# GpSimd splits the first expert's down weights, and VectorE's last two up pieces go behind the block table

## The reference

```python
h = rms_norm(x, norm_mix_g)
qa, ka, va, qb, kb, vb, gates = split(h @ w_in)
ya = swa_sink_attention(qa, ka, va, ...)      # banded, 8 heads
yb = stick_breaking_attention(qb, kb, vb)     # causal, 8 heads
x  = x + (gate_a * (ya @ w_proj_a) + gate_b * (yb @ w_proj_b)) @ w_out
h2 = rms_norm(x, norm_ffn_g)
# top group of 4, then top 2 of its 8 experts
# assignments sorted by expert, each expert padded to blocks of 128 rows
yb = (silu(xr @ w1[e]) * (xr @ w3[e])) @ w2[e]   # for each block of 128 rows
x  = x + segment_sum(yb * row_weight)
```

## Time and profile before

| | |
|---|---|
| median of 3 runs | 2684.91 us (2681.92 to 2688.1) |
| the profiled execution | 2685.95 us, span 2684.1 us |
| TensorE busy | 2586.1 us, 96% of the span |
| VectorE busy | 1638.4 us, 61% |
| ScalarE busy | 1490.5 us, 56% |
| GpSimd busy | 612.9 us, 23% |
| DMA | 536.67 MB, mean 200 GB/s |

### The profile page before, as it was taken

How to read it: one execution, slowest core, us unless ns; L and a number is a source line. 1 busy time by engine, 2 the same in 40 slices (tenths; PEclk the granted TensorE clock), 3 DMA queues, 4 the chain that set the end, 5 groups by cost and what they waited for, 6 DMA issues and landing times. The chain is left out here.

```text
span 2684.1 us, 41247 instructions
## 1 busy us (share of the span) xinstructions
PE 2586.1 (96%) x13573; PEld 2158.1 (80%) x13574; DVE 1638.4 (61%) x2216; ACT 1490.5 (56%) x2628; POOL 612.9 (23%) x707
## 2 busy tenths in 40 slices
PE   7999999989999999999899999699999999999997
PEld 6788777678888888888789998577788888888886
DVE  4400555478777777777543433588766677766673
ACT  4312777567767667676421211358666677766663
POOL 0000111144444444444000000022211222221221
PEclk9999999999999999999899999799999999999999
DMA  6454434586575556543644344479977789877782
GB/s 186 124 206 147 125 127 129 152 273 222 191 215 176 179 185 191 186 149 103 205 164 126 126 126 129 173 274 389 324 231 241 246 277 320 323 236 227 227 303 65
DMA packets 197344, 536.67 MB, mean 200 GB/s; under 512 B 20136, under 2 KB 70776, under 8 KB 192736
## 3 DMA queue, kind: packets, MB, share of 16 engines
q1 hardware_dynamic: 170576, 432.80, 47.1%
q0 software_dynamic: 26640, 102.18, 13.5%
HBM read 403.37 MB, written 131.53 MB: 199 GB/s over the span
## 5 line engine op out<-in xcount | busy, mean ns | idle before, releaser
L1078 POOL TENSOR_TENSOR sb_sig<-sb_sig,sb_R 128x512 f32<-128x512 f32 (+1 forms) x320 | 341.2, 1066 | 410.2 <-DVE sb_R L1018 409.9
L52 PE MATMUL ex_ps_h<-w_region,ex_x_hi 128*128 128x512 f32 x816 | 322.1, 395 | 0.8 <-DVE ex_x_lo L1934 0.8
L54 PE MATMUL ex_ps_h<-w_region,ex_x_lo 128*128 128x512 f32 x816 | 318.3, 390 | 0.0
L53 PE MATMUL ex_ps_h<-w_region,ex_x_hi 128*128 128x512 f32 x816 | 317.9, 390 | 0.0
L1939 DVE TENSOR_TENSOR w_region<-ex_w,w_region 128x1024 fp32r<-128x1024 f32 x248 | 284.7, 1215 | 1.4 <-ACT w_region L1787 1.3
L1018 DVE TENSOR_TENSOR_SCAN sb_R<-sb_z,sb_R,sb_zeros 128x512 f32<-128x512 f32 x192 | 245.6, 1279 | 57.8 <-ACT sb_z L946 57.6
L1944 DVE TENSOR_TENSOR ex_wd_lo<-ex_w,ex_wd_hi 128x1024 fp32r<-128x1024 f32 x200 | 239.3, 1218 | 40.8 <-ACT ex_wd_hi L1794 40.7
L1787 ACT CAST w_region<-ex_w 128x1024 fp32r<-128x1024 f32 x248 | 239.8, 1052 | 8.2 <-DMA ex_w<-in_w_exp 8.2
L958 ACT CAST sb_aT_hi<-sb_pst 128x512 fp32r<-128x512 f32 (+1 forms) x320 | 168.3, 526 | 134.1 <-PE sb_pst L1107 130.8
L1026 DVE TENSOR_TENSOR sb_aT_lo<-sb_pst,sb_aT_hi 128x512 fp32r<-128x512 f32 (+1 forms) x320 | 192.1, 601 | 51.9 <-ACT sb_aT_hi L958 49.8
L945 ACT ACTIVATE sb_sig<-sb_z 128x512 f32<-128x512 f32 (+1 forms) x320 | 172.4, 539 | 85.7 <-PE sb_z L1100 84.3
(11 more groups left out here) (296 smaller groups left out, 6164.4 us busy)
## 6 DMA issues: line engine op xcount, KB each, us to landing
ex_w<-in_w_exp SPq DMA_DIRECT2D x378, 512.0 KB, 9.3
sb_w_hi<-wg_d SPq DMA_DIRECT2D x48, 512.0 KB, 3.6
sb_w_lo<-wg_d SPq DMA_DIRECT2D x48, 512.0 KB, 4.5
gates<-sb_go SPq DMA_DIRECT2D x64, 256.0 KB, 4.0
mo_gates<-gates SPq DMA_DIRECT2D x64, 256.0 KB, 4.1
h<-w_stage POOLq DMA_DIRECT2D x17, 512.0 KB, 2.9
nt_x<-in_x SPq DMA_DIRECT2D x16, 512.0 KB, 4.1
vhl<-nt_vo SPq DMA_DIRECT2D x16, 512.0 KB, 5.1
```

Of the source, the lines that this page charges most:

```text
L52: nc.tensor.matmul(out, w_hi, x_hi, start=first, stop=False)
L53: nc.tensor.matmul(out, w_hi, x_lo, start=False, stop=False)
L54: return nc.tensor.matmul(out, w_lo, x_hi, start=False, stop=last)
L1078: nc.gpsimd.tensor_tensor(sig[:, j % 5, 0:width], sig[:, j % 5, 0:width], R[:, r, first:first + width], ALU.mult).then_inc(a_done, 1)
```

## The change

The four splits of the first expert's down pieces move from VectorE to GpSimd, where they stand between `fetch(0)` and `fetch(1)`. Up piece 6 moves behind `split_x(0)` and the table, in front of up piece 7. VectorE gets one wait, for all four down splits, in front of the loop. The low halves have the same values as before.

```diff
@@ gpsimd
             pool.wait_ge(table_step, FIRST_COLUMN)
             fetch(0)
+            for k in range(KF):
+                pool.wait_ge(down_rounded, k + 1)
+                nc.gpsimd.tensor_tensor(wd_lo[:, 0, k, :], wr[:, KD + k, :], wd_hi[:, 0, k, :],
+                                        ALU.subtract).then_inc(down_split, 1)
             pool.wait_ge(table_step, TABLE)
             pool.wait_ge(x_turned, 1)
             fetch(1)
@@ vector
-            first_up(NEARLY)
             split_x(0)
             table()
-            for j in range(NEARLY + 1, KD):
+            for j in range(NEARLY, KD):
                 first_up(j)
-            for k in range(KF):
-                down_piece(0, 0, k)
+            dve.wait_ge(down_split, KF)
             dve.wait_ge(table_step, BOUNDS)
             all_experts(dve, up_weights, rows)
```

## The result

The changed kernel takes 2697.82 us (median of 5 runs, 2695.46 to 2698.65) against 2684.81 us (5 runs of the kernel before beside it): ratio 1.0046, 95% interval 1.0035 to 1.0056. It is slower: the medians differ by 13.0 us, and the ratio stands for 12.4 us. I had forecast 4.4 us and a range up to 2692.5.

What follows compares the result with a forecast made beforehand. Expert 1's last down piece landing was taken to bind; with turns, block 0 starts +4.9 us, last issue +3.7, landing 1775.5 against 1771.08: +4.4 us on 2684.91, 2689.3 us; range 2683.5 to 2692.5.

Steps and rivals of the forecast that it cites:

- What bounds the kernel, and that a shift at 1775 carries to the end: DMA engines, then TensorE, are full from 1775 on, so a shift of that beginning moves the end as much.
- The exclusion, from one VectorE split of 1.19 us in another stage: Stick-breaking stage: a split beside a GpSimd product took 1.19 us instead of 0.67, so two-input VectorE instructions and GpSimd reads exclude.
- The rival without contention: One-hots and products run side by side unhindered; only the order acts, -0.7 us, 2684.2 us; chance 0.14.
- So they don't share, they take turns: One-hots and GpSimd's products alternate, an instruction at a time; block 0 starts 4.9 us later; chance 0.58.
- The rival in which GpSimd keeps the turn: Four products run in one piece, 1748.05 to 1755.25, before the third L1921; +6.4 us, 2691.3; chance 0.12.
- 1.80 us a product: Each waiting 128 x 1024 GpSimd product: 1.93 us extrapolated from smaller sizes, less 0.13 of start-up; 2.2 at the upper end.
- Landing, from the last issue at 1767.0 to 1775.5, 0.7 us more than before: Expert 1's last down piece: six loads at 400 GB/s, 7.9 us, gather 1.3, first data 2.0, scatter-add to 1775.5.
- Up piece 6 behind the table costs nothing on TensorE but costs in SyncE's queue: Up piece 7 is delayed 1.14 us, harmless to TensorE; expert 1's up piece 6 load joins the down pieces' burst.
- The second gather and the new wait on VectorE have slack: Second gather goes out some 5 us later with 6 us to spare; VectorE's new wait is met before reached.

Runs made afterwards that it cites:

- pool_only: Changed kernel with up piece 6 back at its old place, so only the down splits move to GpSimd; ratio 1.0037 to the kernel before.
- resync: Changed kernel with one wait between GpSimd's gather and its four queued products, none between the products; ratio 1.0036 to the kernel before.
- pool_memset: Kernel before plus four GpSimd memsets behind the first gather, VectorE's first down split waiting for them; ratio 1.0001 to the kernel before.
- pool_late: Changed kernel with GpSimd's four products held until VectorE has written the fourth one-hot pair; ratio 1.0012 to the kernel before.
- gaps_no_add: Kernel before with up pieces 6, 7 and down pieces 0, 1 split in VectorE's idle gaps, without the empty block's scatter-add; ratio 0.9992.
- swap_in: Changed kernel with the two inputs of VectorE's wide one-hot product exchanged; ratio 1.0060 to the kernel before.

## Why the prediction was wrong

- *What bounds the kernel, and that a shift at 1775 carries to the end:* right here. `turn_g(1)` moved by 13.0 us, the end by 13.7.
- *The exclusion, from one VectorE split of 1.19 us in another stage:* right, and it is the main cause: pool_only, with the products alone, loses 8.9 of the 13.7 us. The rival without contention fell.
- *"So they don't share, they take turns":* this step failed. Behind the gather there were no turns, and one one-hot waited for all four products (11.04 us). The two products of the earlier trace rows each had idle time in front of them; no row showed queued ones against VectorE, so the step from "one waits" to "they alternate" had nothing under it. The rival in which GpSimd keeps the turn came true, in a stronger form than I priced: the instruction that was already issued was held too, although I had put it first because it began 0.16 us earlier. The rule that I quoted, whichever is second waits, did not hold here by the recorded starts. My two reasons against this rival (VectorE's instruction has waited since its issue, GpSimd needs its start-up) did not help VectorE. Of the 9.3 us by which block 0 started late 2.6 are this step, the difference to resync.
- *1.80 us a product:* too little. Four queued products take 9.24 us, 2.31 each; +2.0 us for the four. The estimate of 2.25 us, half of what the Trainium skill (GPSIMD Engine Reference, "3.1 Elementwise — side-by-side cycle accounting") gives for an addition of 2048 elements, was nearer than my extrapolation from 128 and 512 elements. The 0.13 us that I took off for a product that waited had no row behind it: the one of the earlier trace rows needed 1.15 us after the split's end, more than its 1.09 alone. resync, which takes turns as I had it, starts block 0 6.7 us late instead of 4.9, and most of these 1.8 us are the longer products.
- *Landing, from the last issue at 1767.0 to 1775.5, 0.7 us more than before:* the other large miss. I counted bytes at 400 GB/s and gave the scatter-add 0.5 us. It came to 5.3 more than before: 3.2 for the scatter-add, and 2.1 for the rest of the burst. Even with turns the kernel would have lost about 10 us (resync: 951.7 against 941.4), not 4.4. So the direction was right, and the sum failed at three places: no turns, longer products, a later landing.
- *Up piece 6 behind the table costs nothing on TensorE but costs in SyncE's queue:* right in kind; 1.1 us of issue alone. The end is 1.7 us later, but `turn_g(1)` only 0.7, and block 0 began at the lower clock in that profile.
- *The second gather and the new wait on VectorE have slack:* right, neither is on the chain.

## What to carry to other kernels

Work moved to GpSimd was not hidden here wherever VectorE read two SBUF operands beside it. Before counting it as free, look at what VectorE has there, instruction by instruction. GpSimd's memsets did no harm (pool_memset), and VectorE's subtraction with one operand in PSUM lost nothing (pool_late). Where both must read, try a wait between an indirect DMA and the GpSimd work behind it, so that an instruction is held by one product at a time. That bounds the loss and doesn't remove it: resync still ends 10.4 us late. And when a chain of waits ends in a load, price the load with what else goes out in the same microseconds, a scatter-add above all, and not by its bytes.

## What the hardware showed that I had not expected

- A VectorE instruction issued before four queued GpSimd products can wait for all of them: 11.04 us for 1.76 (10.51 for 1.22 with a plain subtraction). One wait of 0.2 us between GpSimd's gather and the products cut that to one product at a time.
- TensorE's granted clock at block 0's start differs between the profiles, and I can't say by what. In the changed kernel's profile the first matmul takes 0.49 us (granted clock 1.0, 2.4 GHz). In eight of the fifteen experiments it takes 0.79 us; in one of them, gaps_no_add, the granted clock stayed at 0.50 (1.2 GHz) for the first 3 us of the block. In swap_in, another, the scatter-add went out 1.8 us later than in the changed kernel and the last down piece was rounded 3.0 us sooner; that the second follows from the first is likely by the row of five kernels above, not shown.
- A burst of six 512 KB loads with a gather and a scatter-add in it lands its last piece 13.2 us after the issue (rounded 10.3 to 13.3 us after it in the five profiles that have such a burst). In the kernel before, where one of the six goes out 9 us ahead of the last and the others 1.1 us apart, it is 7.8 us.
